# Staging the gate matrix of a PEER layer in half tiles with double buffers instead of quarter tiles with triple buffers

## The chip, the cores and the metric

The kernel runs on one core of one Trainium2 chip. The metric is the device time of one execution, in microseconds (us); lower is better. The work of the core is spread over five instruction streams: TensorE (PE; its weight loads are shown apart as PEld), VectorE (DVE), ScalarE (ACT), GpSimd (POOL) and SyncE (SP, which here only issues transfers). Sixteen DMA engines move the data. Transfers that SP issues show as the queue "hardware_dynamic", those that POOL issues as "software_dynamic".

## The reference

One inference step of a one-layer decoder trunk: an mLSTM and a stick-breaking attention side by side, an output projection, and then a PEER layer, which retrieves single-neuron experts by product keys. The change touches only the PEER layer:

```python
qry = (xf @ w_query).reshape(T, 8, 2, 128)
sa = einsum('thd,nd->thn', qry[:, :, 0], sub_keys_a)      # 128 keys a
sb = einsum('thd,nd->thn', qry[:, :, 1], sub_keys_b)      # 128 keys b
# per head: top 16 of each, their 256 sums, top 16 of those
experts = 128 * ia + ib;  gates = softmax(top_s)          # T x 128 picks
act = gelu(einsum('tkd,td->tk', expert_u[experts], xf))
y = einsum('tk,tkd->td', gates * act, expert_v[experts])
```

There are T = 1088 tokens (1024 of the prompt, 64 of the samples), D = 1024, and 16384 experts, number 128a + b. All is float32.

## The kernel before

The program is a row of phases, each of which ends with a barrier of all engines before the next begins. The last two are `routing` and `apply`. Tokens come in tiles of 128: tiles 0 to 7 of the prompt, and tile 8 (`NT`) of the 64 sample tokens. Two ways of doing the experts stand side by side. Tiles 4 to 7 (D0 to D1) are "dense": every expert is evaluated for their 512 tokens by matmuls, and the result is weighted with a gate matrix G, which is zero where a token did not pick an expert. Tiles 0 to 3 and 8 are "gathered": each token's picked rows of `expert_u` and `expert_v` are fetched by indirect DMAs.

**routing** computes queries and scores of all nine tiles, picks the experts of the dense tiles and of tile 8, and builds G. It is written as turns j = -1 to 4 of 16 slots; each engine runs through the same turns and slots in its own program order, held together by semaphores. In a turn j from 1 to 4 every slot s builds G for 8 tokens (`GT`) of the dense tile d = j - 1; i = 16d + s numbers these steps 0 to 63. Step i is:

- DVE, `hot(i)` (L2060): two compares of 128x1024 make the one-hots `hot_a` and `hot_b`, in buffer i modulo `NO`. If i >= NO it first waits until PE has finished spread(i - NO), which read this buffer.
- ACT, `gate_a` (L1982): eight activations multiply `hot_a` by the gates, in place.
- PE, `spread(i)` (L1926): eight products, 16 matmul records of 128x128 in the trace, make G for the 8 tokens in the PSUM tile `psG` (two buffers).
- ACT, `keep(i)` (L1990): copies `psG` to `G_stage`, transposed so that a token's number runs innermost, and in the stretch of the current part of the tile.
- SP, `keep` (L1824): when a whole part (`HT` tokens) is in `G_stage`, one DMA writes it to DRAM as `G_d[q]`, of shape 128 (b) x 128 (a) x HT. A buffer of `G_stage` is written again by ACT only after its transfer has landed (`g_stored`).

In the same slots DVE also runs two pieces of the top-16 search of the tile before (L1675 to L1730), and the normalisation of up to two further tiles in a turn: in slots 0 and 8 `norm_sum` (L2032), in the same slot `norm_scale` (L2038, which waits for ACT's `r_rstd`, L1955), and a slot later the transposes. PE does their queries (L1899, with `w_query` loaded in four blocks of 2 MB per tile, L1819, two buffers) in slots 2 to 5 and 10 to 13. The turn ends on DVE with `split`; the next begins with PE's transposes of the picks (L1918) and DVE's copy of them (`kT`, L2052), which `hot` needs. The phase ends when SP has seen the last store landed:

```python
gs = sb("G_stage", [P, NS_, NK, HT])
G_d = dram("G_d", (TD // HT, P, NK, HT))
if i >= NO: dve.wait_ge(g_out, i - NO + 1)          # hot(i)
for i in range(NS_): sp.wait_ge(g_stored[i], ...)   # end of the phase
```

**apply** goes over the 128 values of a. For each, SP loads 128 rows of `expert_u` (`e_u`, 512 KB, three buffers) and of `expert_v` (`e_v`, eight buffers), PE transposes `e_u` (L2282), ACT copies it (L2327), PE makes psH for 512 tokens (L2290), ACT puts it through gelu (L2348), DVE multiplies by G (`weigh`, L2369), and after eight values of a PE makes the sums over experts (L2303), which DVE adds to Y (L2377). G comes back from DRAM in 32 loads of 1 MB, four values of a at once and all 512 tokens, on SP's queue between the loads of `e_u`:

```python
g = sb("e_g", [P, 2, TD // HT, GA, HT])   # GA = 4
sp.dma_start(g[:, i % 2, :, :, :], G_d[:, :, a:a + GA, :].rearrange("q b a t -> b q a t"))
w = W[:, a % NW, :].rearrange("p (q t) -> p q t", t=HT)
```

In DRAM a partition's run without a break is GA x HT numbers. Between these steps, at places fixed in the program order, DVE works through the 576 gathered picks: a dot product with the row of `expert_u` (L2404), then a multiply-add of the row of `expert_v` (L2420). POOL fetches the rows, 128 of 4 KB a pick (`pick_u` L2230 with five buffers, `pick_v` L2238 with four). DVE also runs the top-16 search of the gathered tiles there.

Of the kernel before, what the change touches and what calls it, by code (L numbers as in the profile page):

```python
# [26 lines left out]
P = 128  # L27
# [18 lines left out]
PH, NK, DK, TK = 8, 128, 128, 16  # L46
NE = NK * NK
KX = PH * TK
HT = 32

D0, D1 = 4, 8
TD = (D1 - D0) * P
# [30 lines left out]
def build(nc, io):  # L83
    ctx = ExitStack()
    with ctx:
# [11 lines left out]
        def phase(run, **kw):  # L97

            with ExitStack() as scope:
                scopes.append((scope, []))  # L100
                run(**kw)
                _, held = scopes.pop()
                with nc.Block() as block:  # L103
                    @block.sync
                    def _(sp):
                        for s in held:
                            sp.sem_clear(s)
# [19 lines left out]
        def dram(name, shape, dt=F32):  # L127
            return nc.dram_tensor(name, shape, dt, kind="Internal").ap()
# [9 lines left out]
        with outer:  # L138
# [12 lines left out]
            with nc.sbuf_tensor("cols", [P, NT + 1, P], F32) as cols, \  # L151
# [6 lines left out]
                with nc.sbuf_tensor("hcat_s", [P, D], F32) as hcat_s, \  # L158
# [6 lines left out]
                    phase(sample_attention, **shared)  # L165
        G_d = dram("G_d", (TD // HT, P, NK, HT))
        hf_d = dram("hf_d", (hf_at(NT) + NS, D))
        sc_d = dram("sc_d", (len(GATHER_TILES) - 1, P, 2 * PH, NK))
        with nc.sbuf_tensor("XT", [P, KD, TD], F32) as XT,              nc.sbuf_tensor("ids", [P, 2, KX], I32) as ids,              nc.sbuf_tensor("pick_gates", [P, 2, KX], F32) as pick_gates:
            shared.update(XT=XT, G_d=G_d, hf_d=hf_d, sc_d=sc_d, ids=ids, pick_gates=pick_gates)  # L170
            phase(routing, **shared)
            phase(apply, **shared)
# [115 lines left out]
def load_rows(eng, dst, mod_d, col, sample):  # L288

    if sample:  # L290
        src = mod_d[1:1 + NB, col:col + D].unsqueeze(1).broadcast_to([NB, SQ, D])
    else:
        src = mod_d[0:1, col:col + D].broadcast_to([P, D])
    return eng.dma_start(dst, src)
# [1438 lines left out]


def routing(nc, io, sem, mod_d, x1_d, XT, G_d, hf_d, sc_d, ids, pick_gates, **_):

    NG, GT, NS_, NO = 4, 8, 3, 3  # L1740
    ND = D1 - D0
    ROUND = 1.5 * 2.0 ** 23
    rows = lambda k: P if k < NT else NS
# [16 lines left out]
    with ExitStack() as ctx:  # L1760
# [15 lines left out]
        oa, ob = sb("hot_a", [P, NO, GT, NK]), sb("hot_b", [P, NO, GT, NK])  # L1776
        gs = sb("G_stage", [P, NS_, NK, HT])
        psT, psQ, psS, psG = ps("r_psT", [P, D]), ps("r_psQ", [P, 512]), ps("r_psS", [P, 512]), ps("psG", [P, 2, GT, NK])
# [7 lines left out]
        oa_hot, oa_set, ob_set, g_out, g_kept = sem("oa_hot"), sem("oa_set"), sem("ob_set"), sem("g_out"), sem("g_kept")  # L1786
# [10 lines left out]
        def in_turn(j, s):  # L1797

            return [(asked.index(k), k, s - begin(j, r)) for r, k in enumerate(turns[j])]

        @block.sync
        def _(sp):
            load_rows(sp, gain[:, :], mod_d, 4 * D, False).then_inc(mods_in, 16)
            load_rows(sp, shift[:, :], mod_d, 3 * D, False).then_inc(mods_in, 16)

            def load(i):
                k = asked[i]
                if i >= 2:
                    sp.wait_ge(x_free, i - 1)
                if k == NT:  # L1810
                    sp.wait_ge(x_free, i)
                    load_rows(sp, gain[0:NS, :], mod_d, 4 * D, True).then_inc(mods_in, 16)
                    load_rows(sp, shift[0:NS, :], mod_d, 3 * D, True).then_inc(mods_in, 16)
                sp.dma_start(xp[0:rows(k), i % 2, :], x1_d[k * P:k * P + rows(k), :]).then_inc(x_in[i % 2], 16)

            def load_query(n):
                if n >= 2:
                    sp.wait_ge(q_out, n - 1)
                sp.dma_start(w_q[:, n % 2, :, :], io["w_query"][0, :, n % NG * 512:(n % NG + 1) * 512].rearrange("(k p) n -> p k n", p=P)).then_inc(wq_in[n % 2], 16)  # L1819

            def keep(d, quarter):
                q = d * (P // HT) + quarter
                sp.wait_ge(g_kept, d * (P // GT) + (quarter + 1) * HT // GT)
                sp.dma_start(G_d[q], gs[:, q % NS_, :, :]).then_inc(g_stored[q % NS_], 16)  # L1824

            load(0)
            for n, name in enumerate(("sub_keys_a", "sub_keys_b")):
                sp.dma_start(sub_rows[:, n, :], io[name][0]).then_inc(sub_in, 16)
            load_query(0)
            load_query(1)  # L1830
            load(1)
            for j in range(-1, ND + 1):
                for s in range(SLOTS):
                    for i, k, at in in_turn(j, s):
                        if at == 0 and i + 2 < len(asked) and asked[i + 2] != NT:
                            load(i + 2)
                        if at == 2 and i + 1 < len(asked) and asked[i + 1] == NT:
                            load(i + 1)
                        if at == 1 and not is_dense(k):
                            sp.wait_ge(h_d, i + 1)  # L1840
                            sp.dma_start(hf_d[hf_at(k):hf_at(k) + rows(k), :], hf[0:rows(k), :]).then_inc(hf_kept, 16)
                        if 2 <= at < 2 + NG and NG * i + at < NG * len(asked):
                            load_query(NG * i + at)
                        if at == 3 + NG and not is_dense(k) and k != NT:
                            sp.wait_ge(sc_copied, NG * (i + 1))
                            sp.dma_start(sc_d[GS.index(k), 0:rows(k), :, :], sg[0:rows(k), :, :]).then_inc(sg_kept, 16)
                    if j >= 1 and s % 4 == 3 and s > 3:
                        keep(j - 1, s // 4 - 1)
                if j >= 1:
                    keep(j - 1, P // HT - 1)  # L1850
            sp.wait_ge(hf_kept, 16 * len(GS))
            sp.wait_ge(sg_kept, 16 * (len(GS) - 1))

            sp.wait_ge(made, ND + 1)
            sp.dma_start(ids[NS:P, 0, 0:KX // 2], c.found_i[0:NS, KX // 2:KX]).then_inc(halves_in, 16)
            sp.dma_start(pick_gates[NS:P, 0, 0:KX // 2], c.gates[0:NS, :, :].rearrange("p h k -> p (h k)")[:, KX // 2:KX]).then_inc(halves_in, 16)
            sp.wait_ge(halves_in, 32)
            for i in range(NS_):
                sp.wait_ge(g_stored[i], 16 * len(range(i, ND * P // HT, NS_)))

# [647 lines left out]
```

## Time and profile before

| What | us |
|---|---|
| time of the kernel, median of 3 runs | 4270.66 (4268.82 to 4272.81) |
| the profiled execution's own time | 4266.88 |
| span of its instructions | 4264.8 |
| DVE busy over the span | 2824.8 (66%) |
| PE busy over the span | 3624.0 (85%) |
| POOL busy over the span | 1550.4 (36%) |
| ACT busy over the span | 903.9 (21%) |
| steps of G (first `hot` to last store issued) | 1624.2 to 2101.4 |
| first instruction of apply | 2110.8 |

The shares are means over phases with different limits, so each phase is to be read by its own windows. A wait is put down to what came last by the profile. All times of rows below count from the start of the span.

### The profile page before, as it was taken

What the parts mean: (1) busy time and instruction counts of PE and PEld (TensorE: products, weight loads), DVE (VectorE), ACT (ScalarE), POOL (GpSimd) and SP (SyncE); (2) the same over time, 40 slices, a digit from 0 to 9 for tenths busy, and PEclk for the clock granted to TensorE, in tenths of its full rate; (3) what the DMA queues carried; (4) which work ended last, traced back from release to release, by engine and by line L of the source; (5) the groups of instructions that cost most, each with busy time, mean ns of one, the idle gap of its engine ahead of it and who ended that gap; (6) DMA issues with size and microseconds to landing.
All of it is one profiled execution on the core that took longest, in us unless ns stands there. A gap on an engine that the chain in (4) does not pass through costs nothing.

```text
span 4264.8 us, 40506 instructions
## 1 busy us (share of the span) xinstructions
PE 3624.0 (85%) x13051; PEld 2002.7 (47%) x13051; DVE 2824.8 (66%) x5382; ACT 903.9 (21%) x1895; POOL 1550.4 (36%) x1376
## 2 busy tenths in 40 slices
PE   8799977888759588887498889999999899889995
PEld 1344434555445277887344344444444444444442
DVE  1223224566433157888688898888989888987777
ACT  0111113565412014545311101110011111111110
POOL 1000000000045100000056576666766666666675
PEclk9899986888879789998699999999999999999998
DMA  8211103110155355654399899999999999999997
GB/s 322 109 47 44 49 19 135 49 50 35 23 167 154 112 193 183 252 213 164 141 368 338 330 367 381 389 346 367 377 384 391 374 382 373 350 383 396 388 382 280
DMA packets 371494, 1045.52 MB, mean 245 GB/s; under 512 B 31197, under 2 KB 106013, under 8 KB 366114
## 3 DMA queue, kind: packets, MB, share of 16 engines
q0 software_dynamic: 179728, 649.93, 40.9%
q1 hardware_dynamic: 191570, 393.17, 25.6%
q8 instruction: 99, 1.62, 0.2%
q14 instruction: 97, 0.79, 0.1%
HBM read 975.47 MB, written 67.22 MB: 244 GB/s over the span
## 4 chain that ended last, share of the span: by engine, by line
DVE 16%; DMA 14%; PE 7%; POOL 6%; DVEq 4%; issue 3%; ACT 0%; SPq 0%; POOLq 0%; ACTq 0%
DMA pick_v<-in_expert_v,ids 11%; DVE acc L2420 7%; DVE e_junk L2404 5%; PE psY L2303 4%; DVEq L2415 4%; POOL pick_u L2230 3%; DMA e_u<-in_expert_u 3%; POOL pick_v L2238 3%; PE psH L2290 3%; DVE e_away L1717 1%; DVE e_found L1720 1%; PE psU L2282 0%; DVE e_W L2369 0%; DVEq L1683 0%; DVE e_spare L1678 0%
## 5 line engine op out<-in xcount | busy, mean ns | idle before, releaser
L2290 PE MATMUL psH<-XT,e_uT 128*128 128x512 f32 x2048 | 968.2, 614 | 87.2 <-ACT e_uT L2327 87.2
L2303 PE MATMUL psY<-e_v,e_W 128*128 128x512 f32 x2048 | 889.2, 596 | 19.9 <-DVE e_W L2369 19.8
L2420 DVE SCALAR_TENSOR_TENSOR acc<-pick_v,pick_w,acc 128x1024 f32<-128x1024 f32 x571 | 733.4, 1284 | 243.6 <-DMA pick_v<-in_expert_v,ids 201.9
L2230 POOL DMA_INDIRECT pick_u<-in_expert_u,ids x576 | 721.6, 1253 | 391.0 <-DVE pick_dot L2404 257.6
L2238 POOL DMA_INDIRECT pick_v<-in_expert_v,ids x576 | 665.5, 1155 | 287.9 <-issue 156.4
L2404 DVE CUSTOM_DVE_ANT_0 e_junk<-pick_u,x_rows 128x1024 bf16<-128x1024 f32 x576 | 702.3, 1219 | 25.1 <-DMA pick_u<-in_expert_u,ids 12.5
L2303 PEld LDWEIGHTS psY<-e_v,e_W 128*128 128x128 f32 x2048 | 390.9, 191 | 515.5 <-issue 488.1
L2290 PEld LDWEIGHTS psH<-XT,e_uT 128*128 128x128 f32 x2048 | 381.7, 198 | 479.3 <-issue 375.5
L406 PE MATMUL ps_p<-w_in_sb,hT 128*128 128x512 f32 x1008 | 441.0, 597 | 0.0
L2327 ACT ACTIVATE e_uT<-psU 128x512 f32<-128x512 f32 x256 | 149.5, 594 | 741.8 <-PE psU L2282 741.5
L406 PEld LDWEIGHTS ps_p<-w_in_sb,hT 128*128 128x128 f32 x1008 | 190.6, 191 | 231.5 <-issue 230.8
L1926 PE MATMUL psG<-hot_a,hot_b 128*128 128x128 f32 x1024 | 161.9, 324 | 118.5 <-ACT hot_a L1982 118.5
L2282 PEld LDWEIGHTS psU<-e_ident,e_u 128*128 128x128 f32 x1024 | 134.2, 147 | 224.6 <-issue 135.9
L2203 POOL DMA_DIRECT2D e_scores<-sc_d x4 | 2.4, 596 | 637.9 <-POOLq L103 637.9
L2282 PE MATMUL psU<-e_ident,e_u 128*128 128x128 f32 x1024 | 162.6, 284 | 79.5 <-DMA e_u<-in_expert_u 79.5
L2331 ACT ACTIVATE pick_dot<-pick_dot 128x8 f32<-128x8 f32 x72 | 14.9, 208 | 1001.4 <-DVE pick_dot L2404 1001.3
L1926 PEld LDWEIGHTS psG<-hot_a,hot_b 128*128 128x128 f32 x1024 | 150.8, 234 | 127.6 <-ACT hot_a L1982 127.6
L1164 POOL IOTA s_lane<- 128x1 int32 x1 | 0.1, 133 | 523.1 <-POOLq L103 523.1
L577 POOL MEMSET sel_head<- 4x512 f32 x1 | 0.5, 514 | 517.6 <-POOLq L103 517.6
L1982 ACT ACTIVATE hot_a<-hot_a,kT 128x128 f32<-128x128 f32 x512 | 156.1, 389 | 105.5 <-DVE hot_a L2060 105.4
L1059 DVE TENSOR_SCALAR zb<-psZ,sb_bias_sb 128x128 f32<-128x128 f32 (+7 forms) x64 | 52.3, 817 | 153.8 <-PE psZ L847 151.6
L1899 PE MATMUL r_psQ<-hT_g,w_query_sb 128*128 128x128 f32 (+1 forms) x1280 | 150.1, 279 | 4.6 <-DVE hT_g L2048 3.4
(441 smaller groups left out, 4059.7 us busy)
## 6 DMA issues: line engine op xcount, KB each, us to landing
w_query_sb<-in_w_query SPq DMA_DIRECT2D x36, 2048.0 KB, 8.3
e_u<-in_expert_u SPq DMA_DIRECT2D x128, 512.0 KB, 8.0
e_v<-in_expert_v SPq DMA_DIRECT2D x128, 512.0 KB, 9.9
G_d<-G_stage SPq DMA_DIRECT2D x16, 2048.0 KB, 9.6
e_g<-G_d SPq DMA_DIRECT2D x32, 1024.0 KB, 24.9
w_ada<-in_w_ada SPq DMA_DIRECT2D x12, 2048.0 KB, 8.4
w_in_sb<-in_w_in SPq DMA_DIRECT2D x1, 14368.0 KB, 42.3
pick_u<-in_expert_u,ids POOLq DMA_INDIRECT x576, 9.0
```

The costliest lines, as they stand in the source:

```text
L406: m = pe.matmul(ps_p[n % 4][:, :], hT[:, b, j, :], w_in_sb[:, j, c0:c0 + 512], start=j == 0, stop=j == KD - 1)
L1899: m = pe.matmul(psQ[:, u * P:u * P + rows(k)], w_q[:, n % 2, j, u * P:(u + 1) * P], turned(k, j), start=j == 0, stop=j == KD - 1)
L1926: m = pe.matmul(psG[:, i % 2, t, :], ob[:, i % NO, t, :], oa[:, i % NO, t, :], start=True, stop=True)
L1982: m = act.activation(oa[:, i % NO, t, :], oa[:, i % NO, t, :], ACT.Copy, scale=kT[:, d % 2, 2, n * GT + t:n * GT + t + 1])
L2230: pool.indirect_dma_start(gu[:, i % NGU, :], None, io["expert_u"][0], bass.IndirectOffsetOnAxis(ids[:, q % 2, j:j + 1], 0)).then_inc(pu_in ...
L2238: pool.indirect_dma_start(gv[:, i % NGV, :], None, io["expert_v"][0], bass.IndirectOffsetOnAxis(ids[:, q % 2, j:j + 1], 0)).then_inc(pv_in ...
L2282: t = pe.transpose(psU[:, half, j * P:(j + 1) * P], u[:, a % NU, c * P:(c + 1) * P], ident[:, :])
L2290: m = pe.matmul(psH[a % 2][:, :], uT[:, a % 2, j, :], XT[:, j, :], start=j == 0, stop=j == KD - 1)
L2303: m = pe.matmul(psY[i % NY][:, :], W[:, (b * NBK + t) % NW, k * P:(k + 1) * P], v[:, t, half_cols(half)], start=t == 0, stop=t == NBK - 1)
L2404: dve.tensor_tensor_reduce(junk[:, :], gu[:, i % NGU, :], xg[:, :], 1.0, 0.0, ALU.mult, ALU.add, dot[:, i // PB % 2, i % PB:i % PB + 1]).t ...
L2415: dve.drain()
L2420: dve.scalar_tensor_tensor(out=sums_q, in0=gv[:, i % NGV, :], scalar=wgt[:, m % 2, o:o + 1], in1=sums_q, op0=ALU.mult, op1=ALU.add).then_i ...
```

## The change

`HT` goes from 32 to 64 tokens, `NS_` (buffers of `G_stage`) from 3 to 2, and `NO` (buffers of the one-hots) from 3 to 2. `G_stage` so takes 2 x 32 KB a partition in place of 3 x 16 KB, each of the one-hots 8 KB in place of 12 KB. SP issues a store after slot 11 and after the end of a turn, of 4 MB each, where it issued one of 2 MB after slots 7, 11 and 15 and after the end. In apply `G_d` has 8 parts of 64 tokens, so that a load of `e_g` has runs of 4 x 64 numbers, 1024 bytes, where it had 4 x 32, 512 bytes; its size of 1 MB and the number of loads stay. `weigh` reads 8 runs of 64 in place of 16 of 32. ACT's copy into `G_stage` writes runs of 8 numbers at a distance of 64 in place of 32.

```diff
-HT = 32
+HT = 64
@@ routing
-    NG, GT, NS_, NO = 4, 8, 3, 3
+    NG, GT, NS_, NO = 4, 8, 2, 2
@@ SP in routing
-            def keep(d, quarter):
-                q = d * (P // HT) + quarter
-                sp.wait_ge(g_kept, d * (P // GT) + (quarter + 1) * HT // GT)
+            def keep(d, half):
+                q = d * (P // HT) + half
+                sp.wait_ge(g_kept, d * (P // GT) + (half + 1) * HT // GT)
                 sp.dma_start(G_d[q], gs[:, q % NS_, :, :]).then_inc(g_stored[q % NS_], 16)
-                    if j >= 1 and s % 4 == 3 and s > 3:
-                        keep(j - 1, s // 4 - 1)
+                    if j >= 1 and s == 11:
+                        keep(j - 1, 0)
                 if j >= 1:
                     keep(j - 1, P // HT - 1)
```

## Rows read from the trace of the kernel before

**Rows 1.** Windows by stage: us, busy of each engine (instructions), PEclk, DMA share, GB/s.

```profile
1630.00:2105.00 475.00, 359.60 (x2802) 350.55 (x2800) 391.77 (x1124) 242.00 (x636) 0.00 (x0) 0.87 0.49 183
2112.00:4255.00 2143.00, 1932.48 (x5120) 898.99 (x5120) 1805.87 (x3051) 246.45 (x469) 1399.50 (x1175) 0.95 0.98 368
2340.00:2384.00 44.00, 37.02 (x81) 16.05 (x80) 37.52 (x55) 4.86 (x8) 18.96 (x17) 0.92 0.66 221
```

**Rows 2.** Waits, 1630 to 2111: us in total, times, longest us.

```profile
DVE kT L2052 <- PE r_psT L1918: 20.1, 3, 7.2
DVE hf L2038 <- ACT r_rstd L1955: 11.1, 3, 3.9
DVE hot_a L2060 <- PE psG L1926: 1.2, 2, 0.7
```

**Rows 3.** Timeline of PE, DVE and ACT in turn 1: start us, us, instruction.

```profile
1667.19 1.95 PE L1926 MATMUL psG<-hot_a,hot_b 128*128 128x128 f32 x16
1670.18 1.23 DVE L2060 TENSOR_TENSOR hot_a<-number,kT 128x1024 f32<-128x1024 f32 x1
1677.02 1.95 PE L1926 MATMUL psG<-hot_a,hot_b 128*128 128x128 f32 x16
1684.67 0.20 ACT L1953 ACTIVATE r_rstd<-r_ssq 128x1 f32<-128x1 f32 x1
1685.24 1.28 DVE L2038 SCALAR_TENSOR_TENSOR hf<-r_x,r_rstd,r_gain 128x1024 f32<-128x1024 f32 x1 [3.55 <-ACT r_rstd L1955]
1744.09 0.56 DVE L2052 COPY kT<-r_psT 128x384 f32<-128x384 f32 x1 [6.29 <-PE r_psT L1918]
```

**Rows 4.** Timeline of the same steps in turns 2 and 3.

```profile
1793.71 1.23 DVE L2060 TENSOR_TENSOR hot_a<-number,kT 128x1024 f32<-128x1024 f32 x1
1800.70 1.95 PE L1926 MATMUL psG<-hot_a,hot_b 128*128 128x128 f32 x16
1808.92 1.28 DVE L2038 SCALAR_TENSOR_TENSOR hf<-r_x,r_rstd,r_gain 128x1024 f32<-128x1024 f32 x1 [3.69 <-ACT r_rstd L1955]
1917.91 1.23 DVE L2060 TENSOR_TENSOR hot_a<-number,kT 128x1024 f32<-128x1024 f32 x1 [0.50 <-PE psG L1926]
1925.75 1.95 PE L1926 MATMUL psG<-hot_a,hot_b 128*128 128x128 f32 x16
1933.96 1.28 DVE L2038 SCALAR_TENSOR_TENSOR hf<-r_x,r_rstd,r_gain 128x1024 f32<-128x1024 f32 x1 [3.87 <-ACT r_rstd L1955]
```

**Rows 5.** Timeline, the end of routing and the start of apply.

```profile
2101.83 0.50 SPq L1855 DMA_DIRECT2D ids<-r_found_i  x1
2110.80 0.63 SPq L294 DMA_DIRECT2D e_gate_s<-mod_d  x1
```

**Rows 6.** DMA of 1994 to 2001, one store alone: packets, MB, share; the issue's landing.

```profile
q1 hardware_dynamic: 144, 2.10, 70.9%
...
G_d<-G_stage SPq DMA_DIRECT2D x1, 2048.0 KB, 6.2
```

**Rows 7.** DMA of 4060 to 4070, within a load of e_g: packets, MB, share.

```profile
q0 software_dynamic: 936, 3.41, 88.0%
q1 hardware_dynamic: 937, 0.48, 16.2%
```

**Rows 8.** DMA of 1498 to 1507, a load of w_query: packets, MB, share.

```profile
q1 hardware_dynamic: 1040, 2.10, 65.0%
```

**Rows 9.** DMA issues of the page: KB each, median us to landing.

```profile
e_g<-G_d SPq DMA_DIRECT2D x32, 1024.0 KB, 24.9
```

**Rows 10.** Groups of instructions, 2112 to 4264: busy us, mean ns, idle before, releasers.

```profile
L2420 DVE SCALAR_TENSOR_TENSOR acc<-pick_v,pick_w,acc 128x1024 f32<-128x1024 f32 x571 | 733.4, 1284 | 243.6 <-DMA pick_v<-in_expert_v,ids 201.9 <-issue 2.0
L2282 PE MATMUL psU<-e_ident,e_u 128*128 128x128 f32 x1024 | 162.6, 284 | 79.5 <-DMA e_u<-in_expert_u 79.5
L2369 DVE TENSOR_TENSOR e_W<-e_W,e_g 128x512 f32<-128x512 f32 x128 | 87.8, 686 | 13.3 <-ACT e_W L2348 11.0
L2377 DVE TENSOR_TENSOR Y<-Y,psY 128x512 f32<-128x512 f32 x120 | 81.7, 681 | 10.9 <-PE psY L2303 10.7
```

## The prediction

> **What bounds the kernel now.** I read the windows by stage first, because the change lies in two phases that cannot be limited by the same thing. Over the stretch in which routing builds G, DVE is busy 392 of 475 us, PE 360, ACT 242 and the DMA engines 0.49 of the time [rows 1]; DVE's many short instructions leave little between them, so DVE's program order is the clock of this phase. In apply the DMA engines are 0.98 busy at 368 GB/s over 2143 us, with PE at 1932 and DVE at 1806 [rows 1], and DVE's largest idle time, 201.9 us, ends when a gathered row of `pick_v` lands [rows 10]. So apply is bound by the DMA engines, except in short stretches such as 2340 to 2384, where DVE works on a top-16 search and the DMA share drops to 0.66 [rows 1]. A change that takes time from DVE counts in routing, one that takes time from the DMA engines counts in apply.
>
> Then the waits of routing. DVE waits for PE to free a one-hot buffer twice, 1.2 us in all; it waits 11.1 us in three places for ACT's `r_rstd`, and 20.1 us at three turn starts for PE's transposes of the picks [rows 2]. The first number says that three one-hot buffers are just enough. The other two are slack that a later DVE could use up. The timeline of turns 1 to 3 (slots 5 to 8 and the turn's end) then says how much is missing with two, and the DMA tables of short stretches what a packet costs.
>
> **Two one-hot buffers, turns 1 to 3.** With `NO` = 2, hot(i) needs spread(i-2), not spread(i-3). In slots 2 to 5 PE does queries, one spread after each block, and falls behind DVE: spread(5) runs 1677.02 to 1678.97, while DVE starts hot(7) at 1670.18 [rows 3]. DVE will have to stand still until 1678.97, 8.8 us in all by slot 7 (part of it already at hot(6), which needs spread(4), ended at 1669.14; the waits are one delay that grows, not a sum). Queued behind hot on DVE are the search pieces and the norm of the second tile, all on the path. In turn 2 the same pair is 1793.71 against 1800.70 + 1.95 = 1802.65, 8.9 us; in turn 3 1917.91 against 1925.75 + 1.95 = 1927.70, 9.8 us [rows 4]. PE and ACT are not made later by this as far as slot 7, since they are the late ones; hot(7) still ends ahead of ACT's turn to scale it.
>
> Part is given back at once. In slot 8 DVE now waits for `r_rstd` 3.55, 3.69 and 3.87 us [rows 3, 4], because ACT comes to this norm only at 1684.67 [rows 3]. DVE's sum of squares, moved by 8.8 us, ends near 1684.5, just as ACT comes; DVE arrives at L2038 at 1685.24 - 3.55 + 8.8 = 1690.5 and finds it done. So the wait goes, and 8.8 - 3.55 = 5.3, 8.9 - 3.7 = 5.2 and 9.8 - 3.9 = 5.9 us stay: 16.4 us. From slot 8 on the transposes, queries and spreads of the turn's second half follow DVE's norm, so they move with it; PE, not DVE, ends the turn, and the turn's 6.29 us wait for `kT` [rows 3] does not swallow the delay. It does swallow a smaller shortage in the turn's last slots, if there is one. In turn 4 the program has no queries, so PE waits for DVE there and not DVE for PE; I take nothing. Bounds: 0, if PE ends the turn at its old time after all, and 8.8 + 8.9 + 9.8 = 27.5, if no wait is given back. I take 16.4.
>
> **Stores of 4 MB.** Fifteen of the sixteen old stores lie beside other work, with DMA at 0.49 [rows 1]. A store after slot 11 follows a `w_query` block in SP's order, so that block is not behind it, and the next block is wanted only in the next turn; ACT reuses a half buffer a whole turn later. These I cost at nothing; were a `w_query` block behind one, it would cost up to 5 us in each turn. SP waits for the same last G step at each turn's end as before, and no queue is moved past another. But the last store is on the path: it is issued just ahead of the row at 2101.83, the phase waits for it, and apply starts at 2110.8 [rows 5]. A 2 MB store alone takes 0.709 x 7 = 5.0 us of the sixteen engines and lands after 6.2 [rows 6]; the second 2 MB add 5.0 us. Nothing hides them: DVE and POOL stand before the barrier. Bounds 4 and 6.
>
> **Loads of G in runs of 1024 bytes.** Now 2048 packets of 512 B a load, then 1024 of 1 KB. Within such a load SP's queue shows 0.162 x 10 us x 16 / 937 = 27.7 ns for a packet of 512 B on average [rows 7]; `w_query` shows 0.65 x 9 x 16 / 1040 = 90 ns for one of 2.0 KB [rows 8]. The line between them gives about 49 ns at 1 KB. Each pair merged saves 2 x 27.7 - 49 = 6.4 ns, a load 1024 x 6.4 / 16 = 0.41 us, 32 loads 13 us of all engines. Lower bound 0 (a 1 KB packet costs two of 512 B). Upper: the cheapest byte in the trace, the store's, 0.709 x 7 us x 16 / 2.10 MB = 0.038 ns a byte, or 39 ns, saves 16.7 ns a pair and 34 us. I take the line, as it has the nearest sizes, and since DVE and not DMA limits a few stretches, 12 of the 13 us arrive in the time. Cover gone does not matter here: DMA is the bound.
>
> The Trainium skill ("DMA: Bandwidth & Descriptors", section "Why small descriptors are slow (HBM only)") tells of a fixed overhead of about 3 cycles a packet; with the 850 MHz of its next-door section that is an estimated 3.5 ns a merged pair, 7 us for all loads, and the sum below would be 14 instead of 9. The trace's two sizes ask for more than that.
>
> **The rest at nothing.** `weigh` has the same 512 numbers a partition at 686 ns [rows 10]. ACT's copies write at twice the distance; ACT has half of routing free [rows 1]. If a copy took 0.3 us longer, ACT's late stretches (slots 5 to 8) would pass on perhaps 1 us a turn.
>
> **Sum.** 16.4 + 5.0 - 12 = +9.4 us. The profiled execution took 4266.88 us for a span of 4264.8, and lies 3.8 under the median; on the median the forecast is 4270.66 + 9.4 = 4280. Within 0.2%, 8.5 us, a measurement of this kernel cannot tell it from no change.
>
> **Rivals.**
> - *The loads of G give nothing.* The bytes are the same, and if the engines move 1 KB at the pace of 512 B, or DVE sets apply's pace after all, only the costs stand: 16.4 + 5.0 = +21.4, 4292 us. For it: the queue's share together with POOL's is 1.04 in rows 7, so packets overlap and part of a small packet's cost is hidden. Against: 27.7 ns for 512 B against 90 / 4 = 22.5 ns for as many bytes of the larger packets. The Trainium skill sides with this rival ("DMA: Bandwidth & Descriptors", section "Specifications"): a transfer of 512 B or more already runs at line rate. The trace does not bear that out fully, by the 27.7 ns.
> - *The queue behind e_g clears (faster).* A load of `e_g` takes 24.9 us to land [rows 9], as its packets take turns with POOL's 4 KB ones. With half as many packets it should land after some 13 us, and `e_u`, behind it on SP's queue, sooner. PE's 79.5 us of waiting for `e_u` would shrink, and the DVE idle time that ends with PE or ACT, 11.0 + 10.7 = 21.7 us [rows 10], would go: 9.4 - 21.7 = -12, 4258 us. It decides once apply gives back over 30 us. For it, the size of PE's waits; against, that DMA is full while PE waits, so that what `e_u` gains the gathered rows lose.
> - *The turn's end swallows the stalls.* If PE ended each turn when it does now, the 16.4 would vanish in the 20.1 us of waits for `kT` [rows 2]: 5.0 - 12 = -7, 4264 us, no measurable change. For it, the waits are large enough; against, PE's second block of queries hangs on DVE's norm in slot 8.
>
> **Chances.** The forecast 0.45, with its own range 4274 to 4286; about 0.25 of this lies over the 0.2% line and 0.20 within. No gain from the loads 0.22. Queue clears 0.13. Stalls swallowed 0.15. Something later still, such as a `w_query` block behind a longer store, 0.05. Slower by over 0.2%: 0.25 + 0.22 + 0.05 = 0.52; within: 0.20 + 0.15 = 0.35; faster: 0.13. The range goes from half-way into the faster rival, 4260, to just past the one without gain, 4294.
>
> **What the profile after would show.** Waits of DVE's `hot_a` for PE of some 25 to 30 us in all, at slots 5 to 7 of turns 1 to 3, none in turn 4; the 11.1 us for `r_rstd` nearly gone; the `kT` waits nearly as long as now; the last G step 16 us later, and apply's first instruction 21 us later. From there to the end 12 us less, 32768 packets fewer in all, and `e_g` landing well under 24.9 us. I am wrong if the turns don't lengthen (then the second half did not follow DVE), or if apply changes by over 30 us or not at all.

## The result and the profile after

The changed kernel takes 4276.5 us (median of 20 runs), the kernel before 4268.26 in its 20 runs; the ratio is 1.0022, 95% interval 1.0015 to 1.0029, so 9 us more, within 6 to 12. Forecast were 9.4 us. The sum was right; the parts below show that two of its terms were too small, a cost and a gain, by nearly the same amount.

The end of each turn can be read from DVE's copy of the picks. In the kernel before, the first and the fourth copy, which enclose turns 1 to 3:

```profile
1620.25 0.56 DVE L2052 COPY kT<-r_psT 128x384 f32<-128x384 f32 x1 [8.23 <-PE r_psT L1918]
1993.47 0.56 DVE L2052 COPY kT<-r_psT 128x384 f32<-128x384 f32 x1 [7.25 <-PE r_psT L1918]
```

and the four of the changed kernel:

```profile
1619.56 0.56 DVE L2052 COPY kT<-r_psT 128x384 f32<-128x384 f32 x1 [7.86 <-PE r_psT L1918]
1750.23 0.56 DVE L2052 COPY kT<-r_psT 128x384 f32<-128x384 f32 x1 [4.15 <-PE r_psT L1918]
1880.37 0.56 DVE L2052 COPY kT<-r_psT 128x384 f32<-128x384 f32 x1 [4.15 <-PE r_psT L1918]
2015.92 0.56 DVE L2052 COPY kT<-r_psT 128x384 f32<-128x384 f32 x1 [4.15 <-PE r_psT L1918]
```

Turns 1 to 3 took 373.2 us and now take 396.4, 23.1 more: 6.8, 6.2 and 10.1 by turn (turn 1 was 1744.09 - 1620.25 = 123.8 [rows 3]). The waits of routing in the changed kernel (us in total, times, longest):

```profile
DVE hot_a L2060 <- PE psG L1926: 43.2, 15, 6.4
DVE kT L2052 <- PE r_psT L1918: 20.3, 4, 7.9
```

DVE's waits for a one-hot buffer went from 1.2 us [rows 2] to 43.2 in fifteen places; the waits for `r_rstd`, 11.1 us [rows 2], are gone from the list. Of the waits for `kT` the one of 7.9 us stands ahead of turn 1; the other three are 12.4 us, where they were 20.1 [rows 2]. The mechanism can be watched in turn 1 (start us, us, instruction):

```profile
1676.74 1.95 PE L1926 MATMUL psG<-hot_a,hot_b 128*128 128x128 f32 x16
1678.73 1.23 DVE L2060 TENSOR_TENSOR hot_a<-number,kT 128x1024 f32<-128x1024 f32 x1 [3.56 <-PE psG L1926]
...
1690.33 1.28 DVE L2038 SCALAR_TENSOR_TENSOR hf<-r_x,r_rstd,r_gain 128x1024 f32<-128x1024 f32 x1
```

hot(7) starts as spread(5) ends, and L2038 at slot 8 starts without a wait, where it waited 3.55 us [rows 3]. The forecast said 1690.5; counted from the turn's first copy, which lies 0.7 us earlier here, L2038 starts 0.5 us later than that. At the end of the phase, SP's rows (start us, us), first of the kernel before, then of the changed one:

```profile
2101.40 0.32 SPq L1824 DMA_DIRECT2D G_d<-G_stage  x1
```
```profile
2124.34 0.32 SPq L1824 DMA_DIRECT2D G_d<-G_stage  x1
...
2138.50 0.63 SPq L294 DMA_DIRECT2D e_gate_s<-mod_d  x1
```

The last store is issued at 2124.34 and apply begins 14.2 us later; before it was 9.4 (2101.40 to 2110.80 [rows 5]). So 4.8 us for the second 2 MB. Apply begins 27.7 us later than before and ends 7.5 later: it is 20.2 us shorter in these two profiled executions, 2154.0 against 2133.8. Its window, in the columns of rows 1, and the page's line for the loads of G (KB, median us to landing):

```profile
2138.50:4272.30 2133.80, 1930.88 (x5120) 897.14 (x5120) 1804.67 (x3051) 246.52 (x469) 1396.56 (x1176) 0.95 0.97 370
```
```profile
e_g<-G_d SPq DMA_DIRECT2D x32, 1024.0 KB, 16.4
```

All engines do the same work in less time, and a load of G lands in 16.4 us in place of 24.9 [rows 9]. Within such a load (4066 to 4076; packets, MB, share) SP's queue, in the line below, shows 0.193 x 10 x 16 / 657 = 47 ns for packets of 1 KB, where the line between the two sizes had given 49:

```profile
q1 hardware_dynamic: 657, 0.67, 19.3%
```

### The profile page after: what moved, and what is told of

Read it like the earlier page. It is cut to its first block, busy times and chain, and to the rows that moved or that the text cites. A ratio compares the mean times of both kernels' runs of the same rounds, so it can differ in the third digit from the quotient of the medians.

```text
span 4272.3 us, 40489 instructions
## 1 busy us (share of the span) xinstructions
PE 3635.2 (85%) x13051; PEld 2014.8 (47%) x13051; DVE 2824.2 (66%) x5382; ACT 903.6 (21%) x1895; POOL 1546.8 (36%) x1376
## 4 chain that ended last, share of the span: by engine, by line
DVE 17%; DMA 15%; POOL 9%; DVEq 5%; issue 4%; POOLq 0%
DMA pick_v<-in_expert_v,ids 14%; DVE acc L2420 8%; DVE e_junk L2404 5%; POOL pick_u L2230 5%; POOL pick_v L2238 4%; DVEq L2415 4%; DVE e_away L1717 1%; DVE e_found L1720 1%; DVE e_W L2369 0%; DVE e_ia L1677 0%; DVEq L1683 0%; DVE e_spare L1678 0%; DVE e_va L1680 0%; DMA pick_u<-in_expert_u,ids 0%; DVEq L1676 0%
## 5 line engine op out<-in xcount | busy, mean ns | idle before, releaser
L2230 POOL DMA_INDIRECT pick_u<-in_expert_u,ids x576 | 709.5, 1232 | 378.2 <-DVE pick_dot L2404 240.9
L2404 DVE CUSTOM_DVE_ANT_0 e_junk<-pick_u,x_rows 128x1024 bf16<-128x1024 f32 x576 | 702.6, 1220 | 24.9 <-DMA pick_u<-in_expert_u,ids 12.3
L2282 PE MATMUL psU<-e_ident,e_u 128*128 128x128 f32 x1024 | 160.9, 282 | 25.3 <-DMA e_u<-in_expert_u 25.3
L1899 PEld LDWEIGHTS r_psQ<-hT_g,w_query_sb 128*128 128x128 f32 x1280 | 154.3, 202 | 5.0 <-issue 4.7
## 6 DMA issues: line engine op xcount, KB each, us to landing
e_g<-G_d SPq DMA_DIRECT2D x32, 1024.0 KB, 16.4
```

The lines of the kernel that those rows point to most:

```text
L1899: m = pe.matmul(psQ[:, u * P:u * P + rows(k)], w_q[:, n % 2, j, u * P:(u + 1) * P], turned(k, j), start=j == 0, stop=j == KD - 1)
L2230: pool.indirect_dma_start(gu[:, i % NGU, :], None, io["expert_u"][0], bass.IndirectOffsetOnAxis(ids[:, q % 2, j:j + 1], 0)).then_inc(pu_in ...
L2282: t = pe.transpose(psU[:, half, j * P:(j + 1) * P], u[:, a % NU, c * P:(c + 1) * P], ident[:, :])
L2404: dve.tensor_tensor_reduce(junk[:, :], gu[:, i % NGU, :], xg[:, :], 1.0, 0.0, ALU.mult, ALU.add, dot[:, i // PB % 2, i % PB:i % PB + 1]).t ...
```

## The experiments

Each ratio is to the kernel before, for the experiments on the same chip, with its 95% interval. "Turns" are turns 1 to 3 between the first and the fourth copy of `kT`; "apply" is the time from its first instruction to the end. Both come from the one profiled execution of each kernel, the ratio from all its runs. Four kernels whose loads of G leave the layout as it was (before, no2_only, extra_store, g_split) have apply within 2 us of each other.

| Run | Ratio (interval) | Turns, us | Apply, us |
|---|---|---|---|
| before | 1 | 373.2 | 2154.0 |
| changed kernel | 1.0022 (1.0015 to 1.0029) | 396.4 | 2133.8 |
| no2_only | 1.0054 (1.0041 to 1.0067) | 396.2 | 2154.1 |
| half_no3 | 0.9984 (0.9975 to 0.9993) | 373.3 | 2144.1 |
| extra_store | 1.0015 (1.0006 to 1.0024) | as before | 2155.6 |
| warm_pe | 1.0012 (1.0003 to 1.0021) | 387.9 | 2142.0 |
| view_256b | 1.0264 (1.0245 to 1.0282) | as before | 2260.1 |
| view_1kb | 0.9966 (0.9954 to 0.9977) | as before | 2143.9 |
| view_2kb | 0.9973 (0.9964 to 0.9982) | as before | 2144.7 |
| g_split | 1.0007 (0.9997 to 1.0017) | as before | 2153.7 |
| view_256b_split | 1.0212 (1.0195 to 1.0228) | as before | 2256.0 |
| half_no3_v5 | 0.9965 (0.9953 to 0.9977) | 375.2 | 2137.4 |
| half_ga2 | 1.0255 (1.0241 to 1.0268) | as changed | 2245.8 |
| g_on_act | 1.0551 (1.0533 to 1.0568) | as before | 2390.2 |

### The one-hot buffers alone, and taken back

**no2_only**, the kernel before with

```diff
-    NG, GT, NS_, NO = 4, 8, 3, 3
+    NG, GT, NS_, NO = 4, 8, 3, 2
```

> The kernel before with two one-hot buffers, nothing else changed. Theory A (the one-hot buffers lengthen routing): the three turns grow as in the changed kernel, by about 23 us together, ratio to the kernel before 1.0054, and apply keeps its time. Rival B (the turns grew because of the 4 MB stores and half buffers): no growth, ratio 1.000.

1.0054, and the turns grow to 396.2 us, to a tenth those of the changed kernel, although the stores are 2 MB in three buffers. Its waits of routing (us in total, times, longest):

```profile
DVE hot_a L2060 <- PE psG L1926: 43.2, 15, 6.4
```

**half_no3**, the changed kernel with three one-hot buffers. The 3 KB a partition that lacked came from small tiles:

```diff
-    NG, GT, NS_, NO = 4, 8, 2, 2
+    NG, GT, NS_, NO = 4, 8, 2, 3
-        sub, sub_rows = sb("sub_keys_T", [P, 2, NK]), sb("sub_keys", [P, 2, NK])
+        sub = sb("sub_keys_T", [P, 2, NK])           # sub_rows = oa[:, 0, 0:2, :]
-        number, number_i = sb("number", [P, NK]), sb("number_i", [P, NK], I32)
+        number, number_i = sb("number", [P, NK]), c.found_i
-        kT = sb("kT", [P, 2, 3, P])
+        kT = sb("kT", [P, 1, 3, P])                  # and kT[:, 0] for kT[:, d % 2]
```

> The changed kernel with three one-hot buffers again (room made by letting small tiles share space). Theory A: the turns fall back to their old length, the last store still costs 5 us and apply keeps its gain of 20 us: 15 us less than the kernel before, ratio 0.9964. Rival B (the stores lengthened the turns): the turns stay long, ratio 1.002.

(The copy of `sub_keys` now lies in `oa[:, 0, 0:2, :]`, a one-hot buffer not yet in use.) The turns are back at 373.3 us, so the halves and their stores of 4 MB cost nothing inside the turns. Both runs settle theory A against B. The total, 0.9984, is 7 us less than before, not the 15 expected: that sum took the 20 us of the one profile for apply's gain. With 4.8 us for the last store, 7 + 5 = 12 us is what apply gives here. This kernel is faster than both the kernel before and the changed one.

### The last store

**extra_store**, the kernel before with

```diff
+            sp.dma_start(G_x, gs[:, (ND * P // HT - 1) % NS_, :, :]).then_inc(x_stored, 16)
@@ end of the phase
+            sp.wait_ge(x_stored, 16)
```

> The kernel before with a second store of 2 MB, of the last quarter into an unused place in DRAM, right behind the last store. Theory A (the last store is on the path at its own transfer time): 5 us more, ratio 1.0012. Rival D (the phase's end is set by something else): nothing, ratio 1.000.

1.0015, that is 6 us (3 to 10). From the store's issue to apply:

```profile
2097.99 0.32 SPq L1826 DMA_DIRECT2D G_d<-G_stage  x1
2098.35 0.43 SPq L1853 DMA_DIRECT2D G_x<-G_stage  x1
...
2112.33 0.63 SPq L294 DMA_DIRECT2D e_gate_s<-mod_d  x1
```

That is 14.3 us, where it was 9.4: 2 MB behind the last step are paid in full.

### Why the turns grew by 23 and not by 16

PE's timeline of the changed kernel, turn 3, slots 9 to 11 (start us, us):

```profile
1959.95 2.53 PE L1926 MATMUL psG<-hot_a,hot_b 128*128 128x128 f32 x16 [2.60 <-ACT hot_a L1982]
1962.27 13.75 PE L1899 MATMUL r_psQ<-hT_g,w_query_sb 128*128 128x64 f32 x64
1975.82 3.25 PE L1926 MATMUL psG<-hot_a,hot_b 128*128 128x128 f32 x16
1978.91 7.26 PE L1899 MATMUL r_psQ<-hT_g,w_query_sb 128*128 128x64 f32 x64
```

Sixty-four query products take 13.75 us here and 7.26 in the next block, nearly a factor of two, the ratio of the TensorE's two clocks, 1.2 and 2.4 GHz. The granted clock over the slow block (1962.3 to 1975.8) is 0.50, the lower of the two, and over the next (1979 to 1986) 1.00. Ahead of the slow block PE had stood idle for 6.0 us up to 1951.9 and for 2.6 up to 1960. The same place in the kernel before, after idle times of 1.6 and 4.2 us:

```profile
1943.36 3.78 PE L1926 MATMUL psG<-hot_a,hot_b 128*128 128x128 f32 x16 [4.18 <-ACT hot_a L1982]
1946.93 7.85 PE L1899 MATMUL r_psQ<-hT_g,w_query_sb 128*128 128x64 f32 x64
1954.62 2.00 PE L1926 MATMUL psG<-hot_a,hot_b 128*128 128x128 f32 x16
```

There too the clock was low (0.50 from 1943.4 to 1946.9), but only for a spread of 3.78 us, where the one in warm_pe below takes 2.05, and the head of the block.

These rows part the 23.1 us. The spread ahead of the first block of the second half, counted from the turn's copy of `kT`, starts later than before by 5.8, 5.5 and 4.2 us in turns 1 to 3 (it started at 1694.63, 1818.62 and 1943.36 and now does at 1699.72, 1830.26 and 1959.95): this is the delay by the missing buffer, 15.5 us. The rest, 1.0, 0.7 and 5.9 us, 7.6 in all, arises behind that point, in the spreads and blocks that run longer. **warm_pe** is the changed kernel with

```diff
                     if j >= 1:
                         spread((j - 1) * SLOTS + s)
+                    if 1 <= j < ND and s in (7, 8):
+                        for _ in range(20 if s == 7 else 8):
+                            pe.matmul(psQ[:, 0:P], ident[:, :], ident[:, :], start=True, stop=True)
```

> The changed kernel with extra matmuls that no one reads in slots 7 (20) and 8 (8) of turns 1 to 3, where PE stands idle for VectorE. Theory G (the 4.2 us by which turn 3 grew more than the missing buffer asks, and 1.5 and 0.9 us in turns 1 and 2, are matmuls at the lower clock): turn 3 falls from 135.5 to about 131.5, turns 1 and 2 to about 129.5, ratio to the kernel before 1.0008. Rival (the delay is one of waits): turns unchanged, 1.002.

The same block in its trace, after the matmuls that no one reads (L1948):

```profile
1942.39 4.63 PE L1948 MATMUL r_psQ<-r_ident 128*128 128x128 f32 x40
...
1956.65 2.05 PE L1926 MATMUL psG<-hot_a,hot_b 128*128 128x128 f32 x16 [3.38 <-ACT hot_a L1985]
1958.54 7.26 PE L1899 MATMUL r_psQ<-hT_g,w_query_sb 128*128 128x64 f32 x64
```

Turn 3 falls from 135.5 to 127.7 us, turn 2 from 130.1 to 129.5, turn 1 stays at 130.7. So 8.5 us of the changed kernel's turns go when PE is kept busy, nearly all in turn 3. That is more than theory G expected of turn 3 (7.8 for 4) and less of turn 1 (nothing for 1.5), where the extra products did not do what they were meant to: the block behind them still took 8.31 us. The delays of the three spreads stay, 5.8, 5.5 and 4.5 us, 15.8 in all, so they are not an effect of the clock. The difference 387.9 - 373.2 = 14.7 us is not the price of the buffer alone, as warm_pe also takes away the slow stretch that the kernel before has in turn 3.

In the time of the whole kernel less of this is seen: 1.0022 becomes 1.0012, some 4 us, with intervals that overlap. In warm_pe's profiled execution apply, the same program as in the changed kernel, takes 8 us longer, 2142.0.

### What apply's gain depends on

The three "view" kernels leave routing and the size and number of G's loads alone and read the same bytes as if they lay in parts of another size; the gates are then in wrong places. `weigh` follows with runs of `HV` numbers; in view_1kb DVE's busy time in apply changes by 1 us (1804.7 for 1805.9).

```diff
+        HV = 64        # view_1kb; 16 in view_256b, 128 in view_2kb
+        G_v = G_d.rearrange("q b a t -> (q b a t)").rearrange("(q b a t) -> q b a t", b=P, a=NK, t=HV)
-                    sp.dma_start(g[:, i % 2, :, :, :], G_d[:, :, a:a + GA, :]...)
+                    sp.dma_start(g[:, i % 2, :, :, :], G_v[:, :, a:a + GA, :]...)
```

> The same for parts of 64 tokens, runs of 1024 bytes as in the changed kernel, with routing untouched; gates again in the wrong places. Theory A: the trace's packets of 29.0 and 48.6 ns give 32768 x 9.4 / 16 = 19 us less, ratio 0.9955. If the gain is what the run with three one-hot buffers left, 12 us less, 0.9973. Rival E: 1.000.

> The kernel before, but apply reads the same bytes of G as if they lay in parts of 16 tokens, in runs of 256 bytes: its gates are so in the wrong places, and only its time is of use. Theory A (each packet costs a fixed few ns beside its bytes, and apply is bound by the DMA engines): 131072 packets more or less than twice as many; 8 ns x 65536 / 16 = 33 us if the fixed part is 8 ns, ratio 1.004 to 1.008. Rival E (only bytes count): 1.000.

> The same for parts of 128 tokens, runs of 2048 bytes; gates again in the wrong places. Theory A: 16384 packets of some 88 ns, 90 us of the engines where 119 were: 29 us less, ratio 0.993. Rival F (what counts is e_u waiting behind e_g, and this is mended at 1 KB already): no better than 1 KB.

1 KB runs alone give 0.9966, 14 us less (10 to 20). So apply gains by the layout in which G is read, without any change in routing. With the length of a run the distance from one partition's run to the next grows too, from 16 KB to 32 KB; no run parts the two. 2 KB give no more (0.9973), and 256 B cost 113 us. SP's queue on the pages of before, view_256b, view_1kb and view_2kb (packets, MB, share of 16 engines over the span):

```profile
q1 hardware_dynamic: 191570, 393.17, 25.6%
```
```profile
q1 hardware_dynamic: 257106, 393.17, 26.2%
```
```profile
q1 hardware_dynamic: 158802, 393.17, 25.2%
```
```profile
q1 hardware_dynamic: 142418, 393.17, 25.0%
```

Share times span is the queue's work: 1092, 1144, 1070 and 1063 us. From 512 B to 1 KB it falls by 22 us and the time by 14; from 1 KB to 2 KB by 7 more and the time not at all; at 256 B it rises by 52 and the time by 113. Theory A had the time follow the engines' work one to one; it does not.

The two queues over apply alone, before and in view_2kb, tell where saved work went (packets, MB, share):

```profile
q0 software_dynamic: 168592, 615.85, 75.3%
q1 hardware_dynamic: 104280, 172.77, 22.0%
```
```profile
q0 software_dynamic: 168592, 615.85, 75.4%
q1 hardware_dynamic: 55128, 172.77, 20.7%
```

What the two shares leave of apply's time (a little less than the true idle time where packets of the two overlap) is 58 us before, 71 in view_1kb (75.5 and 21.2%), 84 in view_2kb and 90 in view_256b (72.8 and 23.2%), each to about 2 us. So in these traces, of the 19 us of work that 1 KB takes from SP's queue in apply, 13 come back as time in which the engines stand idle, and all of what 2 KB takes besides. At 256 B SP's queue rises by 50 us, the engines' idle time by 32, and POOL's packets, the same in number and size, take 23 us more.

What does follow, up to a point, are PE's waits for `e_u` (us in total, times, longest), in view_256b and view_1kb:

```profile
PE psU L2284 <- DMA e_u<-in_expert_u: 213.2, 15, 24.0
```
```profile
PE psU L2284 <- DMA e_u<-in_expert_u: 20.4, 2, 20.0
```

79.5 at 512 B [rows 10]. This spoke for theory F, the queue behind `e_g`. **g_split** tests it at 512 B:

```diff
-                    sp.dma_start(g[:, i % 2, :, :, :], G_d[:, :, a:a + GA, :]...)   # a % GA == 0
+                    load_g(i, 0)                  # tokens 0 to 255
+                if a % GA == 1:
+                    load_g(a // GA, 1)            # tokens 256 to 511
```

> The kernel before with each load of G cut into two of 0.5 MB, of 256 tokens each, the second issued one value of a later: the same 65536 packets of 512 bytes, but e_u waits behind half as many at once. Theory A (apply gains by the engines' work saved): nothing saved, ratio 1.000. Theory F (it gains because e_u, behind e_g in SP's queue, comes in time): PE's waits for e_u fall from 79.5 us to about 20, and the time by about 14 us, ratio 0.9966, with routing untouched.

```profile
PE psU L2288 <- DMA e_u<-in_expert_u: 28.2, 8, 20.2
DVE acc L2426 <- DMA pick_v<-in_expert_v,ids: 224.2, 154, 9.1
```

PE's waits for `e_u` fall to 28.2 us as F says, and the time stays: 1.0007. DVE waits 224.2 us for `pick_v` where it waited 201.9 [rows 10]: the rows of `expert_v` come later, by 22 of the 51 us that PE won. In the trace g_split issues its fourth load of G 87 us into apply, as view_1kb does, where before it was 96; at the last load it is at 1940, before was 1942, view_1kb is at 1935. So what an earlier `e_u` wins is lost again by the end. F falls as the cause of the 14 us. The same cut at 256 B:

> The run with runs of 256 bytes, its loads cut in two in the same way; gates in the wrong places. Theory A: as slow as uncut, ratio 1.026. Theory F: a half load lands in about 17 us where a whole one took 34.7, so most of the 112 us goes, ratio under 1.010.

1.0212 for 1.0264: 22 us of the 113 by the ratios, 13 by the medians of five runs each. F expected most of it, A nothing; neither has it.

**half_no3_v5** adds a buffer for the gathered rows of `expert_v` (`NGV` 4 to 5) to half_no3.

> The changed kernel with three one-hot buffers and, in apply, five buffers for the gathered rows of expert_v where there were four. Theory A (apply is bound by the engines' work): DVE's waits for pick_v stay near 200 us and the time stays that of the run with three one-hot buffers, ratio to the kernel before 0.998. Theory H (beyond 1 KB runs the saved engine time is lost because a row of expert_v is asked for only when the fourth before it is spent): those waits fall, DMA share rises to 0.99, and the time falls by a further 10 us or more, ratio 0.996 or less.

0.9965, 15 us under the kernel before and the fastest correct kernel here. DVE's waits for `pick_v` are 205.7 us where half_no3 has 212.9, and the DMA share stays 0.97 in both; so by the ratios it gained some 8 us, with intervals that just touch, but not in the way that H describes.

### Two that told little

**half_ga2** (`GA` 4 to 2 in the changed kernel) and **g_on_act** (loads of G issued by ACT, two values of a ahead).

> The changed kernel with G loaded for two values of a at a time, so that runs are 512 bytes again and the number of loads is 64, of 0.5 MB. Theory A (apply gained by the size of the runs): the gain of 20 us goes, ratio to the kernel before 1.0065. Rival C (apply gained by something else in the new layout, or by chance): apply stays short, ratio 1.002.

> The kernel before, with the loads of G (but for the first two) issued by ACT, in a queue of its own, so that e_u is not behind them. Theory A (the engines are full; order does not matter): within 0.2%, ratio 0.999 to 1.001. Rival F (e_u behind e_g costs time): faster, up to 22 us, ratio 0.995.

Both brought a new wait larger than the effect in question. With `GA` = 2 the two buffers hold four values of a, SP waits 1575 us for a free one (264 in the changed kernel), and `e_u` is behind it in program order; with ACT as issuer G comes too late for DVE. The rows of half_ga2 and g_on_act:

```profile
PE psU L2282 <- DMA e_u<-in_expert_u: 275.4, 37, 25.2
```
```profile
DVE e_W L2372 <- DMA e_g<-G_d: 295.6, 28, 15.1
```

## Why the prediction was right

**What bounds each phase.** Right for routing: a delay of DVE in slots 5 to 8 lengthened the phase, and no2_only shows it alone. For apply, "bound by the DMA engines" is too simple: work taken from them came back in part (1 KB) or not at all (2 KB).

**Two one-hot buffers, 16.4 us.** The mechanism was right slot by slot: the starts at 1678.7 and 1690.3, the wait for `r_rstd` gone, `kT` waits not swallowing it, nothing in turn 4 (107.9 us from the last copy of `kT` to the last store's issue, now 108.4). The delay that it describes is 15.5 us. The turns grew by 23.1, and what the step left out is PE's clock after a longer idle time, 7.6 us; it had put this at nothing without a word. The forecast had `kT` waits "nearly as long as now" and 25 to 30 us of waits for the buffer; they are 4.15 us each, and 43.2. In turn 1 hot(12) waits 0.6 us and hot(15) 2.6 besides the three slots foreseen, and the latter comes out of the wait for `kT` that follows.

**The last store, 5.0 us.** Measured 4.8 in the trace, and 1.0015 when added by itself. The other stores at nothing: half_no3's turns are those of before.

**Loads of G, -12 us.** The price of a 1 KB packet was nearly right, 47 ns for a forecast 49, but a pair merged saves the small difference of two such numbers: 2 x 27.7 - 47 = 8.4 ns gives 17 us where 6.4 gave 13, and the queue's work in apply fell by 19. The step "12 of the 13 us arrive" was wrong as well: of the 19 us of work view_1kb gets 10 in its trace and 14 by its ratio. The two errors nearly cancel. By the ratios apply's gain is 14 us in view_1kb, 12 in half_no3 and 14.7 + 1.3 + 4.8 - 5.1 = 16 in warm_pe; in the changed kernel it is 23.1 + 0.5 + 4.8 - 9.4 = 19. Each has an interval of 3 to 5 us either way, so most of the spread can be noise. The profiles of the first three agree, 2142.0 to 2144.1 us, and only that of the changed kernel, 2133.8, lies apart, though warm_pe and half_no3 run the same program in apply. A single execution is thus a poor measure of the gain, and of the 19 us a few may be luck.

So 23.6 + 4.8 - 19 = 9.4, where the forecast had 16.4 + 5.0 - 12. Seven us too little of cost stood against seven too little of gain: that the total was met so closely is luck. That it lay within the range is less so, as both mechanisms were there.

**The rivals.** "The loads give nothing" fell by view_1kb, and with it the rule of the Trainium skill ("DMA: Bandwidth & Descriptors", section "Specifications") that 512 B are enough for line rate, as far as this kernel goes: here two runs of 512 B cost 55 ns and one of 1 KB 47. The trace agrees with it in its other half: below 512 B the loss is steep. "The queue behind e_g clears" described the waits rightly (79.5 to 25.3 us) but not their worth, as g_split shows. "The turn's end swallows the stalls" fell by no2_only, though 7.7 of the 20.1 us of waits for `kT` were used up.

**What stays open.** Why the DMA engines stand idle for longer as the runs grow from 1 KB to 2 KB, why they do so at 256 B too, and why the profiled apply of the changed kernel is 8 to 10 us shorter than those of warm_pe and half_no3.

## What to carry to other kernels

A buffer that shows 1 us of waiting is not spare: compare each producer's start with the end of the consumer one step less far back, and the stall that a buffer fewer brings can be read off the old trace, together with the waits that it will use up. Add to it what PE's clock does after the longer idle time, here 7.6 us on top of 15.5. Where a layout sets both the staging and the length of the runs that are read back, the two can be tested apart by reading the same bytes in another shape.

## What the runs showed of the hardware

- Runs of 256, 512, 1024 and 2048 bytes in loads of the same bytes changed the kernel's time by +2.6%, 0, -0.3% and -0.3%: the step below 512 B is large, the one above it small, and above 1 KB there was none.
- A block of 64 query products took 13.75 us at a granted clock of 0.50, after PE had stood idle for 6.0 and 2.6 us, and 7.26 us when 28 products that no one reads stood ahead of it. Keeping PE busy so took 8.5 us out of the three turns; the kernel went from 1.0022 to 1.0012.
- Removing 51 us of PE's waits for a transfer while the DMA engines were 0.97 busy brought nothing; DVE's waits for another queue's transfers grew by 22 us.
